# Chunked RWKV scan: which partition half each head's tiles live on, and how its stacked products are issued

## The chip, the cores and the metric

The kernel runs on one core of one Trainium2 chip. The metric is the device time of one execution in microseconds (us). A core has a tensor engine (PE, whose weight loads the profile lists apart as PEld), a vector engine (DVE), a scalar engine (ACT), a general engine (POOL), and SP, which issues transfers. Each engine works through its own queue in order and waits on semaphores.

## What is computed

The reference is a two-layer backbone over 512 tokens (256 of context, 256 latent). Each layer has a bidirectional RWKV-7 mixer, an attention, a Fourier mixer and a SwiGLU. The change touches the RWKV recurrence alone, which runs once in each direction for 8 heads of 64 features:

```python
def step(S, inp):
    r_t, w_t, k_t, v_t, kk_t, b_t = inp
    sa = -jnp.einsum("bhvk,bhk->bhv", S, kk_t)
    S = S * w_t[:, :, None, :] + sa[..., None] * b_t[:, :, None, :] + v_t[..., None] * k_t[:, :, None, :]
    return S, jnp.einsum("bhvk,bhk->bhv", S, r_t)
S, ys = lax.scan(step, state0, xs, reverse=reverse)
```

## The kernel before

All is float32. The kernel is a chain of stages, each a block with one program per engine. The stage `scan` (line 998) stands once in each layer. It does the recurrence in chunks of 64 tokens: 8 steps a layer, two directions `d` = 0 and 1 in each step, side by side. In the second layer the first 4 steps need no output `Y`.

Features are on partitions, two heads to a tile: head 2j on partitions 0 to 63 (`UP`), head 2j+1 on 64 to 127 (`DOWN`), so 4 pairs make 8 heads. PSUM is `BANK`; direction `d` owns four banks, 4d plus `B_L`, `B_LT`, `B_G`, `B_S`. One step does, in PE's order:

- **Gram products** (L1285 to L1291) of the scaled operands `BK` (keys) and `QR` (queries): `B_LT`, `B_L`, `B_G`, for d = 0 and then 1. ACT copies one of them to `LTS` (L1111) and the values to `VF` (L1114, each twice, 128x512). DVE masks them into the inverse's first level `T2` (L1198, L1200), and into `ARB` (L1204, one instruction a head half).
- **Transposes** of `BK` (L1296) and, behind ACT's copy `BK_TOK` (L1105), of `VF` (L1305).
- **Five levels** of the triangular inverse (L1298 to L1324): POOL masks `LM` (L1064), PE multiplies (`x1`), ACT copies `X1` (L1120), PE multiplies twice, DVE subtracts into `T2` (L1212, last level L1217). Between the levels DVE does `gram_out` (L1187) and `keep` (L1177), and the operands and exponents of the next step (L1168 to L1170, L1156, L1157); ACT the exponentials of the next step (L1088 to L1094) and copies of the values (L1129, L1134).
- **The end of the step**: `W` (L1333), the first part of `Y` (L1339), the solve (L1345), the rest of `Y` (L1351) and the new state product (L1360). ACT copies `W` (L1137) and `SA` (L1141, one instruction a head half); DVE adds `Y` (L1236) and updates the state: L1240 multiplies the product by the decay, L1243 adds `SD`, the decayed old state, which POOL made at the start of the step (L1056, L1057).

Three of these products contract over 128 partitions: tiles `QRG`, `STATE_V`, `SA_V`, `BK_TOK` hold, for each of 8 heads, the state, query or `SA` part on `UP` and the Gram, value or key part on `DOWN`. So 8 heads stand side by side in the free dimension (64 partitions x 512), and copies across halves are made one head half at a time. A product of 64 columns out goes to PSUM's upper or lower 64 partitions; L1333 and L1339 alternate between them, L1360 writes all heads to `UP`. A product with a contraction over 64 partitions (`each`, L1254) uses `UP` with `UP` and `DOWN` with `DOWN`, in turn. The profile shows two PE records for each float32 matmul.

Of the kernel before, what the change touches and what calls it, by code (L numbers as in the profile page):

```python
# [26 lines left out]
P = 128  # L27
# [8 lines left out]
HEADS = 8  # L36
# [143 lines left out]
def build_in(ctx, nc, ins, out):  # L180
# [30 lines left out]
    DEC = [sb(f"decay_{d}", [HD, HEADS]) for d in range(NDIR)]  # L211
    DEC_KEPT = [sb(f"decay_kept_{d}", [HD, HEADS]) for d in range(NDIR)]
# [694 lines left out]
    def scratch(*shape):  # L907
# [3 lines left out]
        for i, (mem, at, end) in enumerate(free):  # L911
            if at + n <= end:
# [9 lines left out]
    VF = [scratch(PAIRS, 2, HD) for _ in range(NDIR)]  # L922
    T2 = [scratch(2, PAIRS, HD) for _ in range(NDIR)]
    QRG = [scratch(HEADS, 2, HD) for _ in range(NDIR)]
    STATE_V = [scratch(HEADS, HD) for _ in range(NDIR)]
    SA_V = [scratch(HEADS, HD) for _ in range(NDIR)]
    BK_TOK = [scratch(HEADS, HD) for _ in range(NDIR)]
    ARB = [scratch(HEADS, HD) for _ in range(NDIR)]
    SD = [scratch(HEADS, HD) for _ in range(NDIR)]
# [30 lines left out]
    s_sa_v = [sig(f"values_doubled_{d}") for d in range(NDIR)]  # L960
# [3 lines left out]
    s_add = [sig(f"state_product_decayed_{d}") for d in range(NDIR)]  # L964
    s_ds = [sig(f"state_product_{d}") for d in range(NDIR)]
    s_y_out = [sig(f"y_added_{d}") for d in range(NDIR)]
    s_sd = [sig(f"state_decayed_{d}") for d in range(NDIR)]
# [6 lines left out]
    scan_signals = [s_expo, s_exp, s_init, *s_qr, *s_ops, *s_qr2, *s_gram, *s_lts, *s_gram_out, *s_bk_tok, *s_bk_turned, *s_v_turned, *s_add, *s_v, *s_v_tok, *s_sa_v, *s_lm, *s_x1, *s_x1_out,  # L974
                    *s_tx, *s_t, *s_w, *s_w_out, *s_sa, *s_sa_out, *s_y, *s_ds, *s_y_out, *s_sd, *s_st, *s_first, *s_arb]
# [22 lines left out]
    def scan(context_y):  # L998
# [30 lines left out]
        def of_head(h, half):  # L1029
# [4 lines left out]
        by_head = lambda tile, h: (tile.rearrange("p (j h) t -> p j h t", h=2)[:, :, h] if len(tile.shape) == 3 else  # L1034
                                   tile.rearrange("p (j h) q t -> p j h q t", h=2)[:, :, h])
        pairs = lambda bank, a: BANK[:, bank, a:a + HALF].rearrange("p (j t) -> p j t", j=PAIRS)
        with stage() as block:
            @block.gpsimd
            def _(pool):
# [9 lines left out]
                def step(i, need_y, more):  # L1049
                    t = [tokens(pool, d, i + 1) for d in range(NDIR)] if more else None  # L1050
                    for d in range(NDIR):

                        pool.wait_ge(*at_step(s_st[d], i))
                        pool.wait_ge(*at_step(s_exp, i, 2, d + 1))
                        hold(pool, "pool")
                        nc.gpsimd.tensor_copy(DEC_KEPT[d][:], DEC[d][:])  # L1056
                        s_sd[d].mark(nc.gpsimd.tensor_tensor(SD[d][UP], STATE_V[d][UP], DEC[d][:].unsqueeze(2).to_broadcast([HD, HEADS, HD]), ALU.mult))  # L1057
# [18 lines left out]
            def _(act):  # L1076
                def exps(i, t, d):
# [12 lines left out]
                    nc.scalar.activation(e[:, 2], incl, ACT.Exp, scale=KAPPA)  # L1090

                    act.wait_ge(*at_step(s_sd[d], i))
                    for h, rows in enumerate((UP, DOWN)):
                        last = nc.scalar.activation(DEC[d][:].rearrange("p (j h) -> p j h", h=2)[:, :, h:h + 1],  # L1094
                                                    INCL[d][rows, :, bass.ds(t + (CHUNK - 1), 1)], ACT.Exp, scale=-KAPPA)
                    s_exp.mark(last)

                def step(i, need_y, more):
                    here = [tokens(act, d, i) for d in range(NDIR)]
                    t = [tokens(act, d, i + 1) for d in range(NDIR)] if more else None  # L1100
                    def bk_token_major(d):

                        act.wait_ge(*at_step(s_bk_turned[d], i, 1, 1))
                        act.wait_ge(*at_step(s_ds[d], i))
                        s_bk_tok[d].mark(nc.scalar.activation(BK_TOK[d].rearrange("p g t -> p (g t)"), BANK[:, 4 * d + B_S], ACT.Copy))  # L1105

                    for d in range(NDIR):
                        act.wait_ge(*at_step(s_gram[d], i, 3, 1))
# [4 lines left out]
                        v_here = Z[:, Z_V:Z_V + PAIRS, bass.ds(here[d], CHUNK)]  # L1113
# [24 lines left out]
                    for d in range(NDIR):  # L1138
                        act.wait_ge(*at_step(s_sa[d], i, 1, 1))
                        for h, rows in enumerate((UP, DOWN)):  # L1140
                            last = nc.scalar.activation(by_head(SA_V[d][UP], h), pairs(4 * d + B_LT, 0)[rows], ACT.Copy, scale=-1.0)  # L1141
# [1157 lines left out]
```

## Time and profile before

| | us |
|---|---|
| median of 3 runs | 2362.63 |
| lowest, highest | 2360.34, 2364.29 |
| the profiled execution | 2364.6 |
| its span, first to last instruction | 2362.8 |

The page gives each engine's busy time and groups of instructions by line. The timeline gives instructions in order of time, where equal neighbours stand together as one row with their count, and in brackets the engine's idle time ahead of the row and what ended it. "Windows" give the busy time of each engine in a stretch, and the tensor clock granted in it (1.00 is the higher of its two levels, 2.4 GHz; 0.5 would be 1.2 GHz).

### The profile page before, as it was taken

To read this page: it belongs to the slowest core of one execution; us is meant where nothing else is said; L and a number is where in the kernel's file an instruction comes from. 1 tells how busy PE (TensorE), PEld (TensorE's weight loads), DVE (VectorE), ACT (ScalarE), POOL (GpSimd) and SP (SyncE) were. 2 spreads that over 40 slices of the span, in tenths; PEclk is the share of its full clock that TensorE was granted. 3 is DMA by queue.
4 is the path that set the end of the run, shared out by engine and by line. 5 is a ranking of instruction groups with operands and counts; after the bars stand their busy time and mean duration, and the time that the engine had idled before them with its cause. 6 is when DMAs were issued, how large, how long until landed. Compare 5 with 4: busy or idle time off the path is not lost. (4 is left out here: it accounts for less than half of the span.)

```text
span 2362.8 us, 46800 instructions
## 1 busy us (share of the span) xinstructions
PE 2087.1 (88%) x19559; PEld 1657.3 (70%) x19559; DVE 1169.0 (49%) x1849; ACT 832.9 (35%) x1515; POOL 340.5 (14%) x444
## 2 busy tenths in 40 slices
PE   4886888879989999889998998968888798988998
PEld 2653888843557887668886665748887456988988
DVE  1644778762562333253332216377877435545544
ACT  1343444423442222242221114354443244434432
POOL 1112333301100011010001001043332020010000
PEclk8997999989989999999999998979999899999999
DMA  7425000030111332223226743000001211553553
GB/s 263 152 85 200 1 0 2 1 127 13 36 51 49 92 106 89 72 71 107 90 89 238 282 154 125 27 2 0 1 1 44 96 36 56 170 179 125 185 172 126
DMA packets 144521, 219.40 MB, mean 93 GB/s; under 512 B 6846, under 2 KB 123800, under 8 KB 137216
## 3 DMA queue, kind: packets, MB, share of 16 engines
q1 hardware_dynamic: 142880, 215.74, 26.9%
q8 instruction: 101, 1.65, 0.3%
q0 software_dynamic: 1504, 1.71, 0.2%
q14 instruction: 36, 0.29, 0.0%
HBM read 208.00 MB, written 9.44 MB: 92 GB/s over the span
## 5 line engine op out<-in xcount | busy, mean ns | idle before, releaser
L367 PE MATMUL BANK<-H_high,W_high 128*128 128x512 f32 (+2 forms) x1472 | 524.2, 356 | 70.6 <-ACT H_high L630 32.3
L331 DVE TENSOR_TENSOR W_low<-RING,W_high 128x1024 fp32r<-128x1024 f32 x268 | 328.2, 1234 | 461.9 <-ACT W_high L328 461.9
L368 PE MATMUL BANK<-H_low,W_high 128*128 128x512 f32 (+2 forms) x1472 | 520.0, 353 | 0.0
L369 PE MATMUL BANK<-H_high,W_low 128*128 128x512 f32 (+2 forms) x1472 | 519.0, 353 | 0.0
L328 ACT ACTIVATE W_high<-RING 128x1024 fp32r<-128x1024 f32 x268 | 279.3, 1052 | 613.8 <-PE BANK L369 585.9
L367 PEld LDWEIGHTS BANK<-H_high,W_high 128*128 128x128 f32 (+1 forms) x1472 | 283.8, 193 | 117.0 <-issue 50.5
L368 PEld LDWEIGHTS BANK<-H_low,W_high 128*128 128x128 f32 (+1 forms) x1472 | 284.0, 193 | 38.0 <-issue 1.1
L369 PEld LDWEIGHTS BANK<-H_high,W_low 128*128 128x128 f32 (+1 forms) x1472 | 283.7, 193 | 38.0
L1259 PE MATMUL BANK<-RING,WORK 64*64 64x64 f32 x4096 | 166.4, 220 | 16.7 <-DVE RING L1212 8.8
L1259 PEld LDWEIGHTS BANK<-RING,WORK 64*64 64x64 f32 x4096 | 145.2, 134 | 29.2 <-issue 29.0
L1064 POOL TENSOR_TENSOR WORK<-WORK,masks 128x256 f32<-128x256 f32 x160 | 125.5, 796 | 116.5 <-PE BANK L1259 114.7
L367 PE MATMUL BANK<-hidden_high,W_high 128*128 128x512 f32 (+1 forms) x352 | 122.4, 348 | 12.0 <-PEq L2066 12.0
L368 PE MATMUL BANK<-hidden_low,W_high 128*128 128x512 f32 (+1 forms) x352 | 120.0, 341 | 0.0
L369 PE MATMUL BANK<-hidden_high,W_low 128*128 128x512 f32 (+1 forms) x352 | 120.0, 341 | 0.0
L1259 PE MATMUL BANK<-WORK,RING 64*64 64x64 f32 x2560 | 108.1, 225 | 3.1 <-issue 0.7
L2004 POOL TENSOR_TENSOR merge_tiles<-merge_tiles 128x512 f32<-128x512 f32 (+1 forms) x32 | 33.9, 1068 | 480.7 <-DVE merge_tiles L1986 480.7
L1120 ACT ACTIVATE WORK<-BANK 128x256 f32<-128x256 f32 (+1 forms) x160 | 56.5, 362 | 131.5 <-PE BANK L1259 123.5
L1259 PEld LDWEIGHTS BANK<-WORK,RING 64*64 64x64 f32 x2560 | 93.9, 139 | 8.3 <-issue 6.8
L1212 DVE TENSOR_TENSOR RING<-RING,BANK 128x512 f32<-128x512 f32 x128 | 83.7, 683 | 31.9 <-PE BANK L1259 29.1
L1259 PE MATMUL BANK<-RING 64*64 64x128 f32 (+1 forms) x1536 | 79.5, 263 | 21.1 <-DVE RING L1170 21.1
L367 PEld LDWEIGHTS BANK<-hidden_high,W_high 128*128 128x128 f32 x352 | 67.9, 193 | 34.9 <-issue 27.7
L1259 PEld LDWEIGHTS BANK<-RING 64*64 64x64 f32 x1536 | 75.6, 141 | 22.9 <-issue 21.9
(281 smaller groups left out, 3113.9 us busy)
## 6 DMA issues: line engine op xcount, KB each, us to landing
modulation_weights<-w_mod_dram SPq DMA_DIRECT2D x48, 1024.0 KB, 6.7
RING<-w_in_dram SPq DMA_DIRECT2D x46, 1024.0 KB, 5.9
RING<-w_ffn_in_dram SPq DMA_DIRECT2D x44, 1024.0 KB, 5.1
RING<-w_ffn_out_dram SPq DMA_DIRECT2D x20, 1024.0 KB, 5.1
RING<-w_out_dram SPq DMA_DIRECT2D x8, 1024.0 KB, 5.3
h_high<-H_high SPq DMA_DIRECT2D x2, 2048.0 KB, 7.5
h_low<-H_low SPq DMA_DIRECT2D x2, 2048.0 KB, 13.2
H_high<-h_high SPq DMA_DIRECT2D x2, 2048.0 KB, 11.8
```

The costliest lines, as they stand in the source:

```text
L328: high_ready.mark(nc.scalar.activation(self.part(0, c), self.raw(c), ACT.Copy))
L331: low_ready.mark(nc.vector.tensor_tensor(self.part(1, c), self.raw(c), self.part(0, c).bitcast(FP32), ALU.subtract))
L367: nc.tensor.matmul(out, w[0], x[0], start=start, stop=False)
L368: nc.tensor.matmul(out, w[0], x[1], start=False, stop=False)
L369: return nc.tensor.matmul(out, w[1], x[0], start=False, stop=stop)
L1064: s_lm[d].mark(nc.gpsimd.tensor_tensor(LM[d], LTS[d], lanes(level_mask(d, l)), ALU.mult))
L1120: s_x1_out[d].mark(nc.scalar.activation(X1[d][:, :, cols], pairs(4 * d + B_L, 0)[:, :, cols], ACT.Copy))
L1212: s_t[d].mark(nc.vector.tensor_tensor(T2[d].rearrange("p q j t -> p (q j t)"), T2[d].rearrange("p q j t -> p (q j t)"), BANK[:, 4 * d + B_ ...
L1259: last = nc.tensor.matmul(BANK[rows, bank, at + j * stride:at + j * stride + width], lhs(j)[rows], rhs(j)[rows], start=True, stop=True)
L2004: pool_sig.mark(nc.gpsimd.tensor_tensor(total(m), total(m), gate(u), ALU.add))
```

## The change

State, `SA`, `ARB` and the kept queries become tiles of 128 partitions x 4 pairs: each head's part stays on the half where its products arrive, so they are copied by one instruction of 128 partitions (`QR_KEPT`, `STATE`, `SA`, `ARB`). The Gram copy `GRAM_X` and the values `V_X` hold each head on the other half. Each product over 128 partitions becomes two over 64 that add up in PSUM: one from a head's own half (`OWN`), one from the other (`OTHER`). `side_by_side` issues an `OWN` and an `OTHER` product in turn, always into two banks, so that the four combinations of input half and output half follow each other. `B_LT` and `B_G` are issued so too. Where the two parts of one sum stand in one bank, the second waits for the first (`s_w_1`, `s_y_1`, `s_y_2`, `s_ds_1`, `s_turned_1`). The 128x128 transposes become products of 64x64 with a unit matrix. The state is first added to, then multiplied by the decay in place; `DEC_KEPT`, `SD` and POOL's two instructions go, and ACT makes the decay in levels 4 and 5 (`s_dec`).

```diff
-                        nc.gpsimd.tensor_copy(DEC_KEPT[d][:], DEC[d][:])
-                        s_sd[d].mark(nc.gpsimd.tensor_tensor(SD[d][UP], STATE_V[d][UP], DEC[d][:].unsqueeze(2).to_broadcast([HD, HEADS, HD]), ALU.mult))
...
-                        act.wait_ge(*at_step(s_gram[d], i, 3, 1))
+                        act.wait_ge(*at_step(s_gram[d], i, 3, 2))
...
-                            act.wait_ge(*at_step(s_v_tok[d], i, 1, 1))
-                            s_sa_v[d].mark(nc.scalar.activation(SA_V[d][DOWN].rearrange("p g t -> p (g t)"), BANK[DOWN, 4 * d + B_S], ACT.Copy))
+                            act.wait_ge(*at_step(s_st[d], i))
+                            s_dec[d].mark(nc.scalar.activation(DEC[d][:].unsqueeze(2), INCL[d][:, :, bass.ds(here[d] + (CHUNK - 1), 1)], ACT.Exp, scale=-KAPPA))
...
-                        for h, rows in enumerate((UP, DOWN)):
-                            last = nc.scalar.activation(by_head(SA_V[d][UP], h), pairs(4 * d + B_LT, 0)[rows], ACT.Copy, scale=-1.0)
-                        s_sa_out[d].mark(last)
+                        s_sa_out[d].mark(nc.scalar.activation(SA[d], pairs(4 * d + B_LT, 0), ACT.Copy, scale=-1.0))
...
-                        s_add[d].mark(nc.vector.tensor_tensor(STATE_V[d][UP], BANK[UP, 4 * d + B_S].rearrange("p (g t) -> p g t", g=HEADS),
-                                                              DEC_KEPT[d][:].unsqueeze(2).to_broadcast([HD, HEADS, HD]), ALU.mult))
+                        s_add[d].mark(nc.vector.tensor_tensor(STATE[d], STATE[d], pairs(4 * d + B_S, 0), ALU.add))
                         dve.wait_ge(*at_step(s_add[d], i, 1, 1))
-                        s_st[d].mark(nc.vector.tensor_tensor(STATE_V[d][UP], STATE_V[d][UP], SD[d][UP], ALU.add))
+                        dve.wait_ge(*at_step(s_dec[d], i, 1, 1))
+                        s_st[d].mark(nc.vector.tensor_tensor(STATE[d], STATE[d], DEC[d][:].unsqueeze(2).to_broadcast([P, PAIRS, HD]), ALU.mult))
...
+                OWN, OTHER = (UP, DOWN), (DOWN, UP)
+                def side_by_side(width, *products):
+
+                    last = [None] * len(products)
+                    for j in range(PAIRS):
+                        for x, (bank, at, rows, lhs, rhs, start, stop) in enumerate(products):
+                            for h in range(2):
+                                last[x] = nc.tensor.matmul(BANK[OWN[h], bank, at + j * width:at + (j + 1) * width], lhs(j)[rows[h]], rhs(j)[rows[h]],
+                                                           start=start and (j == 0 or stop), stop=stop and (j == PAIRS - 1 or start))
+                    return last
...
+                        for ins in side_by_side(2 * HD, (bank + B_LT, 0, OWN, lambda j: BK[d][:, j, 0], qr, True, True),
+                                                (bank + B_G, 0, OTHER, lambda j: BK[d][:, j, 1], qr, True, True)):
+                            s_gram[d].mark(ins)
...
+                    s_w_1.mark(side_by_side(HD, w_own(0, True), w_other(1, True))[1])
                     if need_y:
+                        s_y_1.mark(side_by_side(HD, y_own(0, True), y_other(1, True))[1])
+                    pe.wait_ge(*at_step(s_w_1, i, 1, 1))
+                    hold(pe)
+                    one, zero = side_by_side(HD, w_own(1, False), w_other(0, False))
+                    s_w[1].mark(one)
+                    s_w[0].mark(zero)
...
+                        solved, added = side_by_side(HD, (4 * d + B_LT, 0, OWN, lambda j: T2[d][:, 1, j], lambda j: WS[d][:, j], True, True),
+                                                     (4 * d + B_S, 0, OTHER, lambda j: BK_TOK[d][:, 1, j], lambda j: V_X[d][:, j], True, False))
```

The order on PE at the start of a step, before:

```order
L1259 MATMUL BANK<-RING 64x128 x8
L1259 MATMUL BANK<-RING 64x64 x8
L1259 MATMUL BANK<-RING 64x128 x16
L1259 MATMUL BANK<-RING 64x64 x8
L1259 MATMUL BANK<-RING 64x128 x8
L1296 MATMUL BANK<-ident,RING 128x128 x8
L1305 MATMUL BANK<-ident,RING 128x128 x4
```

and after (L1234 is `each`, L1247 `side_by_side`; the first rows are those of d = 0, up to the first transposes):

```order
L1234 MATMUL BANK<-RING 64x64 x8
L1247 MATMUL BANK<-RING 64x128 x16
L1247 MATMUL BANK<-eye_heads,RING 64x64 x16
L1234 MATMUL BANK<-RING 64x64 x8
L1247 MATMUL BANK<-RING 64x128 x16
L1247 MATMUL BANK<-eye_heads,RING 64x64 x24
```

The two wide Gram products of a direction now alternate in one run of 16, and half of the transposes stand between the directions. On DVE the state update stands last in the step, with `Y` ahead of it, before:

```order
L1236 ISA
L1236 TENSOR_TENSOR WORK<-WORK,BANK 128x4x64
L1240 TENSOR_TENSOR WORK<-BANK,decay_kept 64x512
L1243 TENSOR_TENSOR WORK<-WORK 64x512
L1240 TENSOR_TENSOR WORK<-BANK,decay_kept 64x512
L1243 TENSOR_TENSOR WORK<-WORK 64x512
```

and after:

```order
L1212 ISA
L1212 TENSOR_TENSOR WORK<-WORK,BANK 128x4x64
L1215 TENSOR_TENSOR RING<-RING,BANK 128x256
L1218 TENSOR_TENSOR RING<-RING,decay 128x256
L1215 TENSOR_TENSOR RING<-RING,BANK 128x256
L1218 TENSOR_TENSOR RING<-RING,decay 128x256
```

The places are the same; what moved is the layout: each instruction has all 128 partitions and half the elements in each.

## Rows read from the trace of the kernel before

**Rows 1.** Part 1 of the page: busy us, share of the span, instructions.

```profile
PE 2087.1 (88%) x19559; PEld 1657.3 (70%) x19559; DVE 1169.0 (49%) x1849; ACT 832.9 (35%) x1515; POOL 340.5 (14%) x444
```

**Rows 2.** Three steps by windows: length, busy us (instructions) of each engine, clock, DMA.

```profile
322.98:355.58 32.60, 29.22 (x722) 26.98 (x720) 24.49 (x42) 13.73 (x36) 11.71 (x16) 0.95 0.00 0
...
418.34:449.59 31.25, 27.73 (x722) 25.52 (x720) 24.50 (x43) 13.73 (x36) 11.71 (x16) 1.00 0.00 0
...
1633.66:1663.64 29.98, 26.89 (x658) 24.71 (x656) 23.67 (x41) 13.73 (x36) 11.71 (x16) 0.94 0.00 0
```

**Rows 3.** Line L1243 alone: ns least/median/most, first and last start.

```profile
L1243 DVE TENSOR_TENSOR WORK<-WORK x32: 682/684/1358, 258.4 to 1821.5; 64x512 f32<-64x512 f32 x32
```

**Rows 4.** Timeline, end of one step: start us, us, engine, line [idle before].

```profile
315.40 0.61 PE L1272 MATMUL BANK<-RING,WORK 32*32 32x32 f32 x32 [0.66 <-ACT WORK L1120]
...
315.94 1.15 PE L1333 MATMUL BANK<-WORK,RING 128*64 128x64 f32 x32
...
317.95 1.15 PE L1259 MATMUL BANK<-WORK,RING 64*64 64x64 f32 x32
318.68 1.56 ACT L1141 ACTIVATE WORK<-BANK 64x256 f32<-64x256 f32 x4 [1.16 <-PE BANK L1259]
...
321.00 2.08 PE L1360 MATMUL BANK<-WORK 128*64 128x64 f32 x32
321.42 0.42 DVE L1236 TENSOR_TENSOR WORK<-WORK,BANK 128x256 f32 x1 [0.47 <-PE BANK L1351]
...
323.01 3.19 PE L1259 MATMUL BANK<-RING 64*64 64x128 f32 x62
...
324.29 1.35 DVE L1243 TENSOR_TENSOR WORK<-WORK 64x512 f32<-64x512 f32 x1
```

**Rows 5.** Timeline, beginning of the same step.

```profile
291.75 4.64 PE L1259 MATMUL BANK<-RING 64*64 64x128 f32 x96
...
294.32 0.67 DVE L1198 TENSOR_TENSOR RING<-BANK,masks 128x512 f32<-128x512 f32 x1
...
295.03 2.03 DVE L1200 TENSOR_TENSOR RING<-RING,eye_heads 128x512 f32<-128x512 f32 x1
...
297.02 0.60 ACT L1105 ACTIVATE WORK<-BANK 128x512 f32<-128x512 f32 x1 [1.01 <-PE BANK L1296]
...
298.32 0.68 PE L1259 MATMUL BANK<-RING,WORK 64*64 64x64 f32 x16
...
299.42 0.68 PE L1259 MATMUL BANK<-RING,WORK 64*64 64x64 f32 x16 [0.42 <-DVE RING L1200]
```

**Rows 6.** Timeline, fourth and fifth level of that step.

```profile
312.54 0.41 DVE L1157 TENSOR_TENSOR WORK<-WORK 128x256 f32 x1
312.88 1.27 DVE L1212 TENSOR_TENSOR RING<-RING,BANK 128x512 f32<-128x512 f32 x2
...
314.36 0.59 ACT L1134 ACTIVATE WORK<-BANK 64x512 f32<-64x512 f32 x1
...
314.97 0.45 ACT L1120 ACTIVATE WORK<-BANK 128x128 f32<-128x128 f32 x2
```

**Rows 7.** Groups by line over the span: busy us, mean ns of one, idle before.

```profile
L1259 PE MATMUL BANK<-RING,WORK 64*64 64x64 f32 x4096 | 166.4, 220 | 16.7 <-DVE RING L1212 8.8 <-DVE RING L1200 4.6 <-issue 0.6
...
L1187 DVE TENSOR_TENSOR RING<-BANK,masks 64x512 f32<-64x512 f32 x64 | 44.1, 689 | 1.4
...
L1057 POOL TENSOR_TENSOR WORK<-WORK,decay 64x512 f32<-64x512 f32 x32 | 33.6, 1051 | 0.0
...
L1177 DVE COPY RING<-RING 64x512 f32<-64x512 f32 x64 | 31.8, 497 | 1.4
...
L1204 DVE TENSOR_TENSOR WORK<-BANK,masks 64x256 f32<-64x256 f32 x64 | 26.6, 416 | 0.4
...
L1272 PE MATMUL BANK<-RING,WORK 32*32 32x32 f32 x1024 | 24.7, 194 | 19.8 <-ACT WORK L1120 9.6 <-DVE RING L1212 9.3
```

**Rows 8.** Groups by line, stage before the scan, 200.0 to 200.5 us.

```profile
L449 PE MATMUL BANK<-modulation_weights,condition_padded 128*32 128x512 f32 x8 | 1.1, 604 | 1.8 <-DMA modulation_weights<-w_mod_dram 1.8
```

More of the change, by code:

```diff
@@ L921, in build_in @@
     BK = [scratch(PAIRS, 2, HD) for _ in range(NDIR)]
-    VF = [scratch(PAIRS, 2, HD) for _ in range(NDIR)]
+    VF = [scratch(PAIRS, HD) for _ in range(NDIR)]
     T2 = [scratch(2, PAIRS, HD) for _ in range(NDIR)]
[L924 to L929, printed above, removed]
+    QR_KEPT = [scratch(PAIRS, 2, HD) for _ in range(NDIR)]
+    GRAM_X = [scratch(PAIRS, 2, HD) for _ in range(NDIR)]
+    STATE = [scratch(PAIRS, HD) for _ in range(NDIR)]
+    V_X = [scratch(PAIRS, HD) for _ in range(NDIR)]
+    SA = [scratch(PAIRS, HD) for _ in range(NDIR)]
+    BK_TOK = [scratch(2, PAIRS, HD) for _ in range(NDIR)]
+    ARB = [scratch(PAIRS, HD) for _ in range(NDIR)]
     EXPO = scratch(2, PAIRS, HD)
@@ L1284, in step @@
                         hold(pe)
-                        s_gram[d].mark(each(bank + B_LT, 0, 2 * HD, lambda j: BK[d][:, j, 0], qr))
                         s_gram[d].mark(each(bank + B_L, 0, HD, q, lambda j: BK[d][:, j, 0], 2 * HD))
@@ L1290, in step @@
                         hold(pe)
-                        s_gram[d].mark(each(bank + B_G, 0, 2 * HD, lambda j: BK[d][:, j, 1], qr))
-                    for d in range(NDIR):
-                        pe.wait_ge(*at_step(s_add[d], i))
-                        hold(pe)
-                        for j in range(PAIRS):
-                            last = nc.tensor.transpose(BANK[:, 4 * d + B_S, j * P:(j + 1) * P], BK[d][:, j].rearrange("p q t -> p (q t)"), ident[:])
-                        s_bk_turned[d].mark(last)
+                        for ins in side_by_side(2 * HD, (bank + B_LT, 0, OWN, lambda j: BK[d][:, j, 0], qr, True, True),
+                                                (bank + B_G, 0, OTHER, lambda j: BK[d][:, j, 1], qr, True, True)):
+                            s_gram[d].mark(ins)
+                        if d == 0:
+                            pe.wait_ge(*at_step(s_add[0], i))
+                            pe.wait_ge(*at_step(s_add[1], i))
+                            pe.wait_ge(*at_step(s_ops[1], i, 1, 1))
+                            pe.wait_ge(*at_step(s_qr[1], i, 1, 1))
+                            hold(pe)
+                        turned = side_by_side(HD, (B_S + 4 * d, 0, OWN, lambda j: BK[d][:, j, 0], eye, True, True),
+                                              (B_S + 4 * (1 - d), HALF, OTHER, lambda j: BK[1 - d][:, j, 1], eye, True, True))
+                        if d == 0:
+                            s_turned_1.mark(turned[1])
+                            pe.wait_ge(*at_step(s_turned_1, i, 1, 1))
+                            hold(pe)
+                        else:
+                            s_bk_turned[1].mark(turned[0])
+                            s_bk_turned[0].mark(turned[1])
                     for l in range(1, LEVELS):
@@ L1303, in step @@
                             hold(pe)
-                            for j in range(PAIRS):
-                                last = nc.tensor.transpose(BANK[:, 4 * d + B_S, j * P:(j + 1) * P], VF[d][:, j].rearrange("p q t -> p (q t)"), ident[:])
-                            s_v_turned[d].mark(last)
+                            turned = side_by_side(HD, (4 * d + B_S, 0, OTHER, lambda j: VF[d][:, j], eye, True, True))
+                            s_v_turned[d].mark(turned[0])
                         for d in range(NDIR):
```

97 lines of the change are left out of this document (36 added, 61 removed).

## Prediction

> **What bounds the kernel now.** I read part 1 of the page first: PE is busy for 88% of the span [rows 1]. That share is a mean over stages, and the change touches the scan alone, so the next view is the timeline of one step of the scan, taken from one start of the Gram products to the next. L1243, twice in each step, is found 32 times, so there are 16 steps, the first ending near 258 and the last near 1821 us, with the rest of layer one between them [rows 3]. Three steps read as windows say what one costs: 31.25 us with `Y` (12 of the 16), 29.98 without (4), and 32.60 where the granted clock was 0.95 instead of 1.00 [rows 2]. So the scan is about 12 x 31.3 + 4 x 30.0 = 495 us of the 2363, and no DMA bounds it.
>
> I cut the step at three points: Gram products start at 291.75, the first level product at 298.32 [rows 5], `W` at 315.94 and the next Gram products at 323.01 [rows 4] (the step that ends there is the one that began at 291.75): **head** 6.57, **levels** 17.62, **end** 7.07 us, 31.26 in all. In the head PE finishes its Gram products after 4.64 us, but the first level starts 1.9 us later. What is late there is DVE: it runs L1198, then 2.03 us of L1200, and direction 1's first level product starts only 1.10 us after direction 0's [rows 5]; DVE is late because the state update before it ran to 325.64 (324.29 + 1.35), 2.6 us into the next step [rows 4]. In the levels PE, ACT and DVE take turns, and in several of them DVE is late: at 312.88 it starts L1212 as soon as L1157 is off it, with no idle time in front [rows 6]. In the end PE and ACT alternate, and PE is nearly always at work [rows 4].
>
> **What PE pays for a tile.** Each float32 matmul is two records. 16 matmuls that alternate between the two output halves take 1.15 us up to the end of the last, whose latency is 0.22 [rows 4, 7]: 0.93, or 0.47 for 8. L1360, with as many matmuls and elements but one output half only, takes 2.08 [rows 4]. So two tiles run at once where the output halves differ. Four at once are seen too: L449 puts four tiles of 32 output columns beside each other, and its 8 records, 0.60 us each in the mean, are over in 1.1 us, 4.8 us of work in 1.1 [rows 8]. And L1272's last run passes 32 records in 0.61 us, of which 0.19 is the latency of the last [rows 4, 7]: 13 ns a record. What no row shows is two tiles with different input halves and the **same** output half. I take it that they run together, as L449's do: a set of 16 matmuls of `side_by_side` then costs what 8 cost now, 0.47 (4 records in 58 ns, 15 ns each, above the 13 seen). The other end is 0.94, two at a time.
>
> The Trainium skill bears against this: its page TensorEngine Tiling (Array Packing), section Performance Considerations, gives each matmul an overhead of about 60 cycles, which is an estimated 25 ns at 2.4 GHz. By that a set (32 records) would take 0.80 and not 0.47, and the gain would be about 1.7 us a step, 27 in all, a harder case of rival 2. The 13 ns a record of L1272 speak against it here.
>
> The same page, section Restrictions and Gotchas, says that row tiles may not be in the same PSUM bank at one time. The sets always use two banks; no run here shows what else would happen.
>
> **The end, 7.07 now.** `W` and the first `Y` are four sets, in the order W, Y, W, Y: both W's are there after 3 x 0.47 + 0.20 latency = 1.61 (now direction 0's is there after 0.68: a loss of 0.9, which today the `Y` run in front of the solve hides, since PE reaches L1259 only at 317.95, 2.01 after the start). ACT's copy of 0.4 gives 2.05, and the fourth set lies under it. The solve of direction 0 with the first part of the state product is 0.47, and its result is there at 2.77. The copy of `SA` is one instruction instead of two for each direction: 0.38, 0.38 against the 1.56 for four [rows 4]; they end at 3.2 and 3.65. The rest of `Y` is 0.94, from 3.3 to 4.25. The state product is two runs of 8 over both output halves, 0.94 in place of L1360's 1.98, to 5.2. With 0.2 for the first records after each wait: **5.4, a gain of 1.7**.
>
> **The head, 6.57 now.** PE: 0.47 (`B_L`) + 0.87 (`B_LT` and `B_G` as one set of 128 columns; one such product alone takes the same now: 4.64 us are 2 x (0.87 + 0.47 + 0.87) and latency) + 0.47 (transposes) + 0.2 (wait for `s_turned_1`) + 0.47 + 0.87 + 0.2 = 3.55 until ACT may copy direction 1's. Then ACT's `LTS` 0.38 and `VF` about 0.4, `BK_TOK` 0.60 [rows 5], PE's transpose of the values 0.47, and handing over between them: 5.6. DVE must keep up: its state update is 4 x 0.42, as L1236 of the same shape [rows 4], with no POOL instruction beside it. It now takes 0.68, 0.68, 0.68 and 1.35, and ends 1.5 after the Gram products start instead of 2.6. Then L1198 0.67 and L1200, which takes 2.03 beside POOL's L1057 (1.05 each) [rows 5, 7] and should take 0.69. `ARB` is one instruction of 0.42 for two. Direction 1's level product then starts 0.5 after direction 0's and no longer 1.10. **5.6, a gain of 0.97.** What is late next is ACT's chain of three copies behind the second Gram set.
>
> **The levels, 17.62 now.** `gram_out` goes from 2 x 0.689 to one of 0.69, `keep` from 2 x 0.497 to one of about 0.45 [rows 7]: 1.2 us less of DVE in each of levels 1 and 2. I walked the levels with the products at 0.47 for 8, ACT's copy 0.38, DVE's 0.69 and POOL untouched: 3.4, 3.7, 3.4, 4.3 and 1.7 us, which is 0.35, 0.2 and 0.45 less than now in the first three, 0.35 more in the fourth and 0.45 less in the last. The fourth loses, since the gain before it brings its `L1212` forward and direction 1's does not come forward as far, and since the next step's operands and exponents (up to L1157 at 312.54 [rows 6]) still stand ahead of L1212 there. The last gains since ACT's L1134 (0.59) no longer stands ahead of L1120, which waited until 314.97 [rows 6]; the decay there is 0.2. Sum 16.5, **a gain of 1.1**.
>
> Together 1.7 + 0.97 + 1.1 = 3.8 us a step. Without `Y` the end is 5.8 now and 4.3 then (the wait for `s_w_1`, 0.2, is open there), so 3.6. 12 x 3.76 + 4 x 3.6 = 59.5 us. The profiled execution took 2364.6, 2.0 above the median of the three runs; 2364.6 - 59.5 = 2305, and against the median 2303. I say **2304**.
>
> Two edits cost nothing: the decay on ACT replaces L1094, at a time when ACT waits for PE, and PE's 80 matmuls more a step lie in sets that are costed. If their cover goes, the first costs 0.2 a step.
>
> **Rival 1, slower.** Two tiles that share an output half do not run together; the place is every set of `side_by_side`, and the price 0.47 more for each set of 64 columns and 0.87 for each of 128. The end becomes 7.8 (three sets to both W's, 2.8 + 0.2, and the solves 0.94 each, against a state product that is 0.94 shorter), the head 7.9 (two wide sets at 1.75, transposes at 0.94), the levels stay at 16.5: +0.9 a step, +15 us, **2377**. It decides against the change as soon as a set of 16 takes more than about 0.84 us. For it: no row shows the pair. Against it: L449 and L1272, with four tiles.
>
> **Rival 2, half the gain.** The records of a set come slower than 15 ns, say midway to today's 29: 21 ns, 0.68 a set. Four sets of the end and two of the head lie on the path: +1.3 a step, so a gain of 2.5, 40 us, **2323**. For it: L1272's run is only 32 records long.
>
> **Rival 3, the clock.** PE was granted less than full clock in one short stretch in some steps, and such a step is 1.35 us longer [rows 2]. If the new step has such a stretch every time, 16 x 1.35 = 21 us are given back: **2325**. For it: PE works less in each step and waits for ACT's chain in the head. Against: the steps as a whole shorten by as much as the work does.
>
> **The numbers.** Forecast as stated, give or take 15 us (each of the three gains wrong by a quarter): 0.62. Rival 2 or 3, or both in part, 2318 to 2345: 0.23. Rival 1: 0.11. A gain well over 75 us: 0.04. The range, 2286 to 2345, holds the first two. A measurement of this kernel can tell 0.2% (4.7 us) from no change. Faster 0.86, same 0.03, slower 0.11.
>
> **What would show it.** Right: steps of 27.5 us; a set of 16 matmuls of 64 columns at a spacing of about 0.47 us; the Gram products of a step begun 5.4 after `W`; L1179, the new L1200, near 0.69 and not 2.03; POOL without a state instruction. Wrong: sets at 0.9 us (rival 1), 0.7 (rival 2), windows of a step with a clock below 1.00 in nearly all of them (rival 3), or DVE without idle time ahead of L1177 in the head, which would mean that the state update still sets the head.

## The result: slower by 1.8%, and the profile after

The changed kernel took 2404.68 us (median of 4 runs, 2402.31 to 2409.67), the kernel before beside it 2361.78 (4 runs, 2360.34 to 2364.29): a ratio of 1.0183, interval 1.0165 to 1.0202. The forecast was 2304, the range ended at 2345, and even the slower rival stood at 2377. The spans of the two profiled executions are 2407.5 and 2362.8 us, so 44.7 us have to be found.

Part 1 of the page of after, against [rows 1], and from part 3 of both pages the queue that carries instructions (packets, MB, share of the DMA engines), first after, then before:

```profile
PE 2071.7 (86%) x22247; PEld 1642.9 (68%) x22247; DVE 1075.5 (45%) x1753; ACT 774.1 (32%) x1419; POOL 298.1 (12%) x380
...
q8 instruction: 172, 2.82, 0.5%
```

```profile
q8 instruction: 101, 1.65, 0.3%
```

Every engine has less work than in [rows 1]: PE 15 us less, DVE 93, ACT 59, POOL 42. None of them became the bound by being busy for longer. What grew is the code that was brought in while the kernel ran: 71 packets more, of 16 KB each.

Next, windows of after (columns as in [rows 2]): a step with `Y` in the middle of the first scan's first loop, the first trip of its second loop, the scan's last step, a step without and one with `Y` of the second scan, the whole first and second scan from first to last state update, and all that comes behind.

```profile
296.19:334.11 37.92, 27.38 (x896) 25.22 (x896) 18.42 (x37) 10.09 (x30) 8.97 (x12) 0.91 0.02 4
371.36:404.82 33.46, 25.39 (x893) 23.31 (x892) 18.12 (x37) 10.20 (x30) 8.79 (x12) 1.00 0.01 4
483.22:515.37 32.15, 26.10 (x895) 24.10 (x891) 14.40 (x29) 8.22 (x24) 7.22 (x10) 0.95 0.02 4
1665.53:1692.58 27.05, 23.20 (x807) 21.48 (x805) 17.74 (x34) 10.09 (x30) 9.10 (x12) 0.99 0.00 0
1751.71:1788.28 36.57, 27.57 (x896) 24.88 (x896) 18.41 (x36) 10.09 (x30) 8.97 (x12) 0.95 0.02 4
259.57:515.37 255.80, 191.49 (x6272) 177.02 (x6272) 124.99 (x245) 68.84 (x204) 61.40 (x82) 0.91 0.02 4
1637.25:1858.40 221.15, 181.90 (x5992) 168.00 (x5988) 122.73 (x238) 68.77 (x204) 61.34 (x82) 0.94 0.01 2
1858.40:2407.50 549.10, 488.49 (x3400) 430.23 (x3400) 266.75 (x409) 215.42 (x338) 32.82 (x46) 0.95 0.39 128
```

The same three long stretches of the kernel before:

```profile
258.44:479.74 221.30, 198.25 (x5049) 182.75 (x5047) 165.99 (x287) 93.67 (x242) 80.01 (x110) 0.98 0.00 1
1603.63:1820.15 216.52, 193.51 (x4850) 178.33 (x4848) 165.18 (x280) 93.66 (x242) 80.22 (x110) 0.97 0.00 1
1820.15:2362.80 542.65, 483.12 (x3402) 424.96 (x3400) 268.00 (x409) 215.58 (x338) 32.90 (x46) 0.95 0.40 129
```

The first scan is 34.5 us longer, the second 4.6, the stages behind it 6.5; what lies ahead of the first scan and between the two is 0.9 shorter together. That makes the 44.7. And the scans differ in kind. A step with `Y` takes 36.6 to 40.0 us in the middle of a loop, with PE busy for only 27.4 of 37.9: it idles for 10.5 us, where it idled for 3.5 in [rows 2]. A step without `Y`, in the same kernel and with the same layout, takes 27.05, for a forecast of 26.4. The last columns tell them apart: 4 GB/s of DMA against 0. The traffic in the slow step, in the step without `Y` and its neighbours (1637.25 to 1720.19 us, where a queue other than q8 carried the one packet), and in two steps of the kernel before:

```profile
q8 instruction: 9, 0.15, 1.6%
```

```profile
DMA packets 1, 0.01 MB, mean 0 GB/s; under 512 B 0, under 2 KB 0, under 8 KB 0
```

```profile
DMA packets 0, 0.00 MB, mean 0 GB/s; under 512 B 0, under 2 KB 0, under 8 KB 0
```

So in after the steps with `Y` bring in packets of instructions, 9 in this one and 7 to 10 in the others, and a step of before brings in none (once 1) except where the loop over steps changes its body, where 5 or 6 come in. Where the step loses its time, by the timeline of PE in after (start us, us, engine, line, what, [idle before, what ended it]) and by its waits over that step (us in total, times, longest):

```profile
299.46 0.62 PE L1234 MATMUL BANK<-RING 64*64 64x64 f32 x14 [3.60 <-issue]
...
302.67 1.22 PE L1247 MATMUL BANK<-RING 64*64 64x128 f32 x17 [2.08 <-issue]
```

```profile
PE BANK L1234 <- issue: 3.9, 2, 3.6
PE BANK L1247 <- issue: 3.6, 3, 2.1
```

The Gram products start 3.60 us late, and the second set, in the middle of a run of matmuls that wait for no engine, stops for another 2.08. "issue" means that PE waited for nothing that the profile shows. In all these are 7.5 us of the step; DVE, ACT and POOL wait for PE meanwhile.

### The profile page after: what moved, and what is told of

It reads as the page before. It is cut to its first block and busy times, and to the rows that moved or that the text cites. A ratio compares the mean times of both kernels' runs of the same rounds, so it can differ in the third digit from the quotient of the medians.

```text
span 2407.5 us, 51837 instructions
## 1 busy us (share of the span) xinstructions
PE 2071.7 (86%) x22247; PEld 1642.9 (68%) x22247; DVE 1075.5 (45%) x1753; ACT 774.1 (32%) x1419; POOL 298.1 (12%) x380
## 3 DMA queue, kind: packets, MB, share of 16 engines
q1 hardware_dynamic: 142880, 215.74, 26.4%
## 5 line engine op out<-in xcount | busy, mean ns | idle before, releaser
L367 PEld LDWEIGHTS BANK<-H_low,W_high 128*128 128x128 f32 (+1 forms) x1472 | 284.2, 193 | 37.9 <-issue 1.1
L1234 PE MATMUL BANK<-RING,WORK 64*64 64x64 f32 x4096 | 170.4, 220 | 12.1 <-issue 4.1
L1234 PEld LDWEIGHTS BANK<-RING,WORK 64*64 64x64 f32 x4096 | 146.8, 135 | 21.8 <-issue 21.2
L1247 PE MATMUL BANK<-RING 64*64 64x128 f32 (+1 forms) x1920 | 89.1, 291 | 10.7 <-issue 8.6
L1234 PE MATMUL BANK<-WORK,RING 64*64 64x64 f32 x2048 | 86.9, 220 | 2.8 <-issue 0.8
L1247 PEld LDWEIGHTS BANK<-RING 64*64 64x64 f32 x1920 | 74.8, 164 | 14.9 <-issue 14.8
L1234 PE MATMUL BANK<-RING 64*64 64x64 f32 x512 | 28.7, 263 | 58.0 <-issue 31.1
```

What stands on the lines that cost most here:

```text
L367: nc.tensor.matmul(out, w[0], x[1], start=False, stop=False)
L1234: last = nc.tensor.matmul(BANK[rows, bank, at + j * stride:at + j * stride + width], lhs(j)[rows], rhs(j)[rows], start=True, stop=True)
L1247: last[x] = nc.tensor.matmul(BANK[OWN[h], bank, at + j * width:at + (j + 1) * width], lhs(j)[rows[h]], rhs(j)[rows[h]], start=start and (j ...
```

## The experiments

**Theory.** PE's loop body for a step with `Y` grew from 368 to 448 matmuls, transposes counted in. At 448 it is no longer kept from one trip of the loop to the next, so PE fetches it again in every trip and stands still meanwhile; the new layout itself is as fast as forecast. **Rivals.** The layout causes the stalls in another way (banks, tiles side by side, the order of the waits); or the gain was never there.

These counts are those of the code. The expectations below give each of them seven lower (361, 441 and so on): 361 is half of the 722 PE records of [rows 2], but each of before's 16 transposes has one record and not two, while after does that work with matmuls of two. The loop body of before is 1440 records of PE and PEld together, that of after 1792 with `Y` and 1600 without.

### 1. The changed kernel with a loop over three levels

PE's part of levels 1 to 3 becomes a loop of three trips. The work is the same, but the body holds 352 matmuls with `Y` and 304 without. Direction 1's values are transposed behind level 3 instead of ahead of it, and the wait for `ARB` stands in every level.

```diff
-                    for l in range(1, LEVELS):
-                        if l in (1, 3):
...
+                    turn_values(0)
+                    trips = Signal.trips
+                    Signal.trips = 3 * trips
+                    with pe.Fori(1, 4) as l:
+                        level(l, False)
+                    Signal.trips = trips
+                    turn_values(1)
+                    level(4, False)
+                    level(5, True)
```

> The changed kernel, with PE's first three levels of the inverse written as one loop of three trips (the values of direction 1 are turned after it): the same matmuls are executed in nearly the same order, but a step's body on PE shrinks from 441 matmuls to 345 (345 is below the 361 of the kernel before). Theory 1 (PE's loop body with Y, 441 matmuls, is too long to be kept, so its code is fetched again in every step and PE stands still for it): instruction packets of 16 KB vanish inside the loops, steps with Y take 27 to 28.5 us and not 37, the total is 2300 to 2325 us. Theory 2 (the new order of the W and Y sets and their waits cost the time in steps with Y): no difference, 2400 to 2410 us. Theory 3 (lower clock takes the time): steps stay over 33 us, as the clock follows from the same work.

Measured: 2338.42 us (4 runs, 2335.04 to 2342.64) against 2364.96 of before, ratio 0.9889 (0.9873 to 0.9906). That is slower than the 2300 to 2325 expected of this run, though the step came out as expected. The change turns from 1.8% slower to 1.1% faster by how PE's code is written. Windows: a step with `Y` and one without, the first step of the loop's second body in each scan, both scans, and the stages behind:

```profile
287.59:315.61 28.02, 24.89 (x905) 23.39 (x903) 18.53 (x37) 10.21 (x30) 9.13 (x12) 1.00 0.00 0
1611.23:1638.84 27.61, 23.25 (x800) 21.43 (x801) 18.18 (x34) 10.21 (x30) 9.13 (x12) 1.00 0.00 0
344.66:374.74 30.08, 24.74 (x878) 22.90 (x874) 18.53 (x37) 10.21 (x30) 8.86 (x12) 1.00 0.01 3
1667.54:1699.95 32.41, 26.53 (x907) 24.81 (x904) 18.68 (x36) 10.21 (x30) 9.09 (x12) 0.97 0.01 3
259.47:461.76 202.29, 177.54 (x6265) 166.32 (x6261) 125.84 (x244) 69.44 (x204) 61.22 (x82) 0.98 0.00 1
1583.06:1784.59 201.53, 172.72 (x5991) 160.91 (x5988) 124.95 (x239) 69.44 (x204) 61.94 (x82) 0.98 0.00 1
1784.59:2332.90 548.31, 488.88 (x3400) 429.88 (x3400) 266.93 (x409) 215.69 (x338) 32.88 (x46) 0.96 0.39 128
```

The step is 28.0 us, where after had 37.9, and its clock is 1.00 instead of 0.91. Of the 11 steps with `Y` in the two scans 8 have 1.00, one 0.97 and two 0.94; in after they have 0.83 to 1.00. So most of after's lower clock came with PE standing still.

### 2. The same loop in the kernel before

The same edit on the old kernel (272 matmuls with `Y`, instead of 368).

```diff
+                    with pe.Fori(1, 4) as l:
+                        level(l, False)
...
+                    turn_values(1)
+                    level(4, False)
```

> The kernel before, with the same loop of three trips on PE: body 265 matmuls instead of 361, nothing else changed. Theory 1: the body of before is kept already, so nothing is gained; the loop's branches may cost up to 0.3 us a step, total 2362 to 2368 us. If the loop alone were a gain whatever the body's length (another reason than code length), this kernel would be faster than before by as much as the other one against the changed kernel.

Measured: 2364.47 us, ratio 0.9997 (0.9987 to 1.0007). The step is as long as the 31.25 of [rows 2]:

```profile
291.74:323.03 31.29, 27.67 (x722) 25.51 (x720) 24.54 (x42) 13.71 (x36) 11.66 (x16) 1.00 0.00 0
```

So the loop has no worth and no cost of its own, within 0.13%, where the code is small enough anyway, and the gain of experiment 1 does not come from it.

### 3 and 4. The kernel before with 80 more matmuls, written out and in a loop

Direction 0's first product of level 1 (8 matmuls) is repeated ten times more. It writes what is there already, so nothing else changes. Once the 80 matmuls are written out, which gives the old kernel the 448 of after (1760 records for 1792):

```diff
+                                if l == 1 and d == 0:
+                                    for _ in range(10):
+                                        x1()
```

> The kernel before, with the first level product of direction 0 repeated ten times more (80 matmuls, 2.3 us of PE work a step), written out: the body with Y is as long as that of the changed kernel (441 matmuls), the one without Y is 409. The result is not altered. Theory 1: steps with Y pay some 4 to 8 us beyond the padding's own 2.3 us and show 8 or 9 instruction packets each; steps without Y (409) pay 2.3 only if 409 is still kept. Theory 2 or 3: every step pays 2.3 us and no more, about 2400 us in all.

and once they stand in a loop of ten trips (376 matmuls in the code, 448 run):

```diff
+                                if l == 1 and d == 0:
+                                    with pe.Fori(0, 10):
+                                        x1()
```

> The same 80 matmuls a step as in the padded kernel, executed by a loop of ten trips over 8: the work is the same, the body is only 369 and 337 matmuls long. Theory 1: no instruction packets inside the loops, every step costs about 2.3 to 3 us more than before, about 2400 to 2410 us, and the difference to the written-out one is the price of fetching: 12 steps less two last ones, x 5 us, some 50 us. Theory 2 or 3: the same time as the written-out one within 5 us.

Measured: 2485.91 us and 2445.75 us (one run each). The second was expected at 2400 to 2410: the expectation priced the 80 matmuls at 2.3 us a step, and their 160 records of 29 ns are 4.6. Windows of the first: a step with `Y`, one without (416 matmuls) that fetched its code, and one without that brought in a single packet, with the traffic of the first two:

```profile
307.24:351.19 43.95, 34.28 (x876) 31.90 (x875) 23.26 (x42) 13.72 (x36) 11.29 (x16) 0.95 0.02 4
1710.98:1751.85 40.87, 33.22 (x818) 31.00 (x816) 22.42 (x40) 13.72 (x36) 11.28 (x16) 0.92 0.01 3
1751.85:1786.49 34.64, 31.59 (x818) 29.49 (x816) 23.67 (x41) 13.73 (x36) 11.64 (x16) 0.95 0.00 0
```

```profile
q8 instruction: 10, 0.16, 1.7%
```

```profile
q8 instruction: 7, 0.11, 1.1%
```

Windows of the second, a step with `Y` and one without, and the traffic of the step with `Y`:

```profile
303.23:340.33 37.10, 33.88 (x882) 31.66 (x880) 24.49 (x43) 13.73 (x36) 11.64 (x16) 0.95 0.00 0
1682.38:1717.05 34.67, 31.55 (x818) 29.45 (x816) 23.68 (x40) 13.73 (x36) 11.64 (x16) 0.95 0.00 0
```

```profile
DMA packets 0, 0.00 MB, mean 0 GB/s; under 512 B 0, under 2 KB 0, under 8 KB 0
```

The same 448 matmuls run in both, with the old layout and without any step in which four tiles work. Written out they cost 6.9 us more in the step with `Y` (43.95 against 37.10); over the kernel it is 40 us, for some 50 expected. In the step without `Y` it is 6.2 where 7 packets came in and nothing where one did. The waits of PE in the slow step are of the kind seen in after:

```profile
PE BANK L1259 <- issue: 4.7, 2, 3.0
PE BANK L1343 <- issue: 1.9, 1, 1.9
```

That is 6.6 of the 6.9 us. The rival that the layout makes the stalls falls with this pair: the old layout has them as well, as soon as the code has that length.

What costs time here is not that code is brought in, but when. The next rows are two neighbouring steps with `Y` of the written-out kernel, the first trip of the second loop and the trip behind it:

```profile
393.62:429.51 35.89, 32.61 (x882) 30.27 (x880) 23.81 (x43) 13.73 (x36) 11.65 (x16) 1.00 0.01 3
429.51:471.53 42.02, 35.31 (x882) 32.89 (x880) 23.24 (x43) 13.73 (x36) 11.30 (x16) 0.92 0.01 4
```

The first trip, which PE reaches without jumping back, brings in 7 packets of q8 and has no wait on "issue" at all. The second brings in 9 and has 3.5 us of it. So here the standstill comes with the jump back to the start of a body that is no longer there.

### 5. Sixteen matmuls fewer: where the edge is

The same with eight repeats instead of ten: 432 matmuls with `Y` (1696 records), and 400 without (1568).

```diff
-                                    for _ in range(10):
+                                    for _ in range(8):
```

> The kernel before, with the first level product of direction 0 repeated 8 times more, written out (64 matmuls, 1.9 us of work a step): the bodies are 425 matmuls with Y, 393 without. The changed kernel showed no packets in its loop with 393 and 9 a step with 441; the padded one with 409 in the second layer had 8 in one of three steps. If the code length decides: the steps without Y have no packets and take about 33 us; those with Y have 8 or 9 packets and over 39 us if 425 is too long, or 34 to 35 us if it is still kept. The result is not altered.

Measured: 2469.04 us (one run). A step with `Y` and one without, and the traffic of the first and of the stretch 1674 to 1773 us, which holds only steps without `Y`:

```profile
308.36:350.83 42.47, 35.17 (x850) 32.46 (x848) 22.38 (x43) 13.84 (x36) 11.27 (x16) 0.92 0.02 3
1707.64:1740.97 33.33, 30.61 (x786) 28.48 (x784) 23.67 (x40) 13.73 (x36) 11.66 (x16) 0.95 0.00 0
```

```profile
q8 instruction: 9, 0.15, 1.7%
```

```profile
DMA packets 0, 0.00 MB, mean 0 GB/s; under 512 B 0, under 2 KB 0, under 8 KB 0
```

Over all kernels, by records of PE and PEld: bodies of up to 1600 (after without `Y`) were kept in every trip, the one of 1632 brought in 7 packets in one step of three and 2 and 1 in the others, and those of 1696, 1760 and 1792 were lost in every trip.

### 6. One loop instead of two

All engines run the 8 steps as loops of 4 and 3 trips and a last step written out by itself. Here PE alone runs one loop of 8 trips in layer one and two of 4 in layer two, so fewer bodies are fetched for the first time.

```diff
-                run(pe, step)
+                for first, end, need_y in (((0, STEPS, True),) if context_y else ((0, N, False), (N, STEPS, True))):
+                    Signal.trips = end - first
+                    with pe.Fori(first, end) as i:
+                        step(i, need_y, True)
+                    Signal.trips = 1
```

Once on experiment 1's kernel:

> The kernel with the level loop, and in addition PE runs its 8 steps of a scan in one loop (first layer) or two of four trips (second layer) instead of two loops and a last step written out: 3 bodies of PE code in the program for 6, the same matmuls. In the kernel with the level loop 5 instruction packets come in at each change from one body to the next, and the step in which that happens takes 30.1 and 32.4 us against 28.1. If PE's code fetching costs there too: 2 to 4 us less for each of the changes that go, total 2326 to 2336 us against 2338. If those steps are long for another reason (clock, the first Y): no difference.

Measured: 2335.05 us (4 runs, 2321.16 to 2336.86), ratio 0.986 (0.9824 to 0.9895), too wide to tell it from experiment 1. Together with the same edit on the kernel before (with experiment 2's loop) it was run once more:

> The changed kernel with both loops on PE, measured again in more rounds, since one of its four runs was 2321 us and the others 2334 to 2337. Expected 2333 to 2337 us, 0.986 to 0.988 of before, and no instruction packet of PE inside the loops.

> The kernel before with both loops on PE, the level loop and one or two loops for the steps of a scan: the control for the fastest version. If the loops alone were worth something, it would be faster than before by more than 0.1%. Theory 1 expects little: before's code is kept inside its loops, and its steps at a change of body took 31.5 and 32.9 us against 31.3, so 2358 to 2365 us, and the gain of the fastest version comes from the change itself.

Measured: 2331.18 us (4 runs, 2329.12 to 2332.65), ratio 0.9866 (0.985 to 0.9883), for 2333 to 2337 expected, and 2362.49, ratio 0.9994 (0.9984 to 1.0004). Windows of the first: a step with `Y`, one without, the first step of the second body in layer two, and both scans:

```profile
316.92:344.93 28.01, 24.88 (x904) 23.38 (x902) 18.54 (x37) 10.21 (x30) 9.13 (x12) 1.00 0.00 0
1608.63:1635.81 27.18, 23.32 (x800) 21.58 (x801) 17.77 (x35) 10.21 (x30) 9.14 (x12) 1.00 0.00 1
1664.77:1694.64 29.87, 25.67 (x922) 24.02 (x922) 18.54 (x36) 10.21 (x30) 9.14 (x12) 1.00 0.01 3
260.71:457.18 196.47, 175.02 (x6270) 164.51 (x6265) 125.90 (x245) 69.49 (x204) 62.22 (x82) 0.99 0.00 0
1581.46:1777.76 196.30, 171.58 (x5984) 160.24 (x5984) 123.65 (x239) 69.51 (x204) 62.22 (x82) 0.98 0.00 1
```

Fewer bodies take 5.8 and 5.2 us off the two scans of experiment 1's kernel, and the span is 5.9 shorter (2327.0 for 2332.9). The worth of this edit is not shown firmly: the times of the second set do not overlap experiment 1's (up to 2332.65, from 2335.04), those of the first set do (up to 2336.86), and the intervals of the ratios overlap as well. In the kernel before it gives nothing measurable. By its median this is the fastest version: 33 us under the kernel before it was run with.

### 7. Are four tiles at once real?

Experiment 1's kernel with `side_by_side` issuing one product behind the other, instead of both in turn. All instructions are the same; two tiles are at work at a time.

```diff
-                    for j in range(PAIRS):
-                        for x, (bank, at, rows, lhs, rhs, start, stop) in enumerate(products):
+                    for x, (bank, at, rows, lhs, rhs, start, stop) in enumerate(products):
+                        for j in range(PAIRS):
```

> The kernel with the level loop, but side_by_side issues all matmuls of its first product and then all of the second, so that two tiles run at a time and not four; the same matmuls, the same code length. If four tiles really run at once in the sets (0.47 us for 16): the narrow sets take 0.94 and the wide ones 1.75, steps with Y 31.5 to 33 us and not 28.1, total 2385 to 2410 us. If the gain of the sets came only from the layout of the copies: no difference, 2338.

Measured: 2366.8 us (one run), 28 more than experiment 1. A step with `Y`, by its window:

```profile
291.67:322.32 30.65, 27.89 (x904) 26.54 (x901) 18.53 (x37) 10.31 (x30) 9.12 (x12) 0.94 0.00 0
```

The step is 2.6 us longer, less than the 3.4 to 4.9 expected (the total was expected at 2385 to 2410), and a part of it is the clock, 0.94 against 1.00. But the set itself shows the effect: the 32 records of the first transposes start 27 ns apart here (323.49 to 324.33 us), and 15 ns apart in experiment 1 (288.51 to 288.98). And with the products no longer in turn the whole gain of the layout over the kernel before is gone (2366.8 against 2364.7): four tiles at once are real, and the gain rests on them.

### 8. Was it POOL that made DVE late?

Experiment 1's kernel with a POOL instruction of the removed one's size put back behind the state update, in a tile that nobody reads, and DVE's wait for it before the next state update.

```diff
+                    for d in range(NDIR):
+                        pool.wait_ge(*at_step(s_st[d], i))
+                        hold(pool, "pool")
+                        s_sd[d].mark(nc.gpsimd.tensor_tensor(SD[d][UP].rearrange("p (j h) t -> p j h t", h=2), STATE[d][UP].unsqueeze(2).to_broadcast([HD, PAIRS, 2, HD]),
...
+                        dve.wait_ge(*at_step(s_sd[d], i, 1, 1))
```

> The kernel with the level loop, with an instruction of 64x512 on POOL for each direction behind the state update, as the kernel before had one (here it multiplies the state by itself into a tile that nobody reads), and the wait of the next state update for it. The theory of the head says that DVE's state and first-level instructions get slower beside it (0.42 to about 0.8, 0.69 to 1.3 or 2.0) but that the chain over ACT's three copies has up to about 1 us to spare over DVE: steps 0 to 1 us longer, total 2338 to 2356 us. If DVE alone set the head before, the step loses about 1.5 to 2 us, 2362 to 2370 us.

Measured: 2339.24 us (2 runs), ratio 0.9893 (0.9873 to 0.9912), the same as experiment 1. DVE's groups over the first scan (busy us, mean ns of one) in experiment 1's kernel, the copy of the Gram products (there L1179, which was L1200 in [rows 5]) and the state's multiply, and then the same two with the POOL instruction back:

```profile
L1179 DVE TENSOR_TENSOR RING<-RING,eye_heads 128x512 f32<-128x512 f32 x14 | 9.7, 692 | 0.5
...
L1218 DVE TENSOR_TENSOR RING<-RING,decay 128x256 f32<-128x256 f32 x16 | 6.8, 425 | 0.5
```

```profile
L1186 DVE TENSOR_TENSOR RING<-RING,eye_heads 128x512 f32<-128x512 f32 x14 | 13.4, 960 | 0.5
L1226 DVE TENSOR_TENSOR RING<-RING,decay 128x256 f32<-128x256 f32 x16 | 11.7, 733 | 0.5
```

```profile
319.70:347.71 28.01, 24.87 (x906) 23.39 (x904) 19.65 (x36) 10.20 (x30) 11.57 (x14) 1.00 0.00 0
```

POOL does slow DVE, by 268 and 308 ns an instruction, and the step is 28.01 all the same: in the new layout DVE has that much to spare. Taking POOL's instruction out was worth nothing that can be measured here (0.8 us between the medians).

## Why the prediction was wrong

**The step that failed** is this one: "Two edits cost nothing: [...] PE's 80 matmuls more a step lie in sets that are costed." Their time on PE was costed; their code was not. The step's body on PE went from 368 to 448 matmuls, and PE did not keep it: 7 to 10 packets of 16 KB come in during each step with `Y`, and in the step shown PE stands still for 7.5 us. None of the three rivals held this either. The slower rival put the loss in tiles that would not run together, and the one on the clock saw the lower clock as a thing by itself.

How much it cost: 2404.68 against 2338.42 of experiment 1, **66 us** for the same work (the kernel before beside them differs by 3). By steps it is 37.9 against 28.0. Of these 9.9, 7.5 are PE's waits on "issue"; the rest, I take it, is the clock (0.91 against 1.00), which I have not measured apart. The old layout paid 6.9 for nearly the same length of code (experiments 3 and 4). That after paid more may be because its sets get through a packet of code in half the time (15 ns a record for 29), so that less of the fetching lies beside work. In line with that, the first trip of the second loop (371.36 to 404.82 us in after), which the padded kernel passes without a standstill, has 5.1 us of "issue" in after; no run tests it apart.

A look at the kernel before would have hinted at it. The views of its trace give 0 packets in a step inside a loop and 5 or 6 in the first step of a body, so that its 1440 records come in as 6 packets, or 96 KB. The Trainium skill has a size to hold 80 more against: its page Advanced Engine Details and Errata, section ISA Cache, gives TensorE 128 KB, in lines of 16 KB with 256 instructions. The packets here have that size and the trace agrees so far: after's 1792 records and the 56 waits, counts, branches and register instructions that its trace has for PE in that step are 1848 instructions, an estimated 7.2 lines of that page or 116 KB. That would still fit in the 128 KB, and it was not kept: the edge to go by is the measured one, between 1600 records and 1696. The page is not refuted by this, since a trip brings in up to 10 packets, more than its 128 KB hold; why it brings in more than the body has is open.

**The terms of the sum**, by the timeline of PE in experiment 1's kernel, cut at the same places as in [rows 4, 5]: Gram products, the transposes of the first set, first level product, and the next Gram products:

```profile
287.17 0.62 PE L1234 MATMUL BANK<-RING 64*64 64x64 f32 x14
...
288.51 0.69 PE L1247 MATMUL BANK<-eye_heads,RING 64*64 64x64 f32 x32
...
293.04 1.15 PE L1234 MATMUL BANK<-RING,WORK 64*64 64x64 f32 x32
```

```profile
315.19 0.62 PE L1234 MATMUL BANK<-RING 64*64 64x64 f32 x14
```

`W` starts at 309.62 in the same timeline.

- **A set of 16 matmuls, 0.47 us**: right. The transposes are 32 records in 0.69, of which 0.22 is the latency of the last. The 25 ns that the prediction estimated from the Trainium skill (TensorEngine Tiling (Array Packing), section Performance Considerations) was rightly set aside as the spacing of such records: 15 ns were measured.
- **Head 5.6**: 5.87. One reason given for it made no difference, though: DVE's L1179 does fall to 0.69, but experiment 8 puts it back to 0.96 in the mean (at most 1.13) at no cost. ACT's chain of three copies is what is late, as was said; whether it would have hidden the 2.03 of [rows 5] too no run shows.
- **Levels 16.5**: 16.6. **End 5.4**: 5.6, and without `Y` 4.7 for 4.3.
- **Step 27.5**: 28.0 with `Y`, against the 31.25 of [rows 2]; 27.2 to 27.6 without, for 26.4.
- **59.5 us in all**: this does not hold even without the fetching. Experiment 1's 2338.42 would have been inside the range, but its gain is 26.5 us. The two scans' windows (14 of the 16 steps) are shorter by 19.0 and 15.0 us in experiment 1's kernel and 24.8 and 20.2 in experiment 6's, where the forecast's share of them is 52.1. Of the 7 us missing in the latter, steps of 28.0 for 27.5 and 27.2 for 26.4 account for all (7.9); in the former 11 us more are missing, of which the steps in which a new body is fetched (30.1 and 32.4 instead of 28) are 6.5, and three steps at a clock of 0.92 to 0.94 (29.05 and 29.46 with `Y`, 28.70 without) 3.6. The two steps ahead of the windows were forecast to gain 7.4 together and gave 1.5 in experiment 1's kernel, with what else lies in those stretches, and in experiment 6's those stretches are 2.7 longer.
- **What lies behind the scans** was taken as untouched, and is 4.5 to 6.6 us longer than before's 542.65 in every kernel with the new layout (547.1 to 549.3); with the old one it is 541.7 to 545.3, the last of these with the 80 matmuls in a loop. It is the same with the code written out and in a loop, so the length of the body does not explain it. Two stretches hold most of it, and the last of them (2310.0 to 2362.8 us in before, 2352.1 to 2407.5 in after) shows of what kind it is: 407 matmuls in both, PE busy for 46.17 and 48.78 us, the clock 0.99 in both. So the matmuls themselves come more slowly, and PE does not wait longer. Why is **open**: no run tests it. The tiles of the scan became smaller, and no run shows whether that moved what these stages read.

**Clock.** Rival 3 was about a stretch below full clock in each step. In experiment 1's kernel the clock is 1.00 in 8 of 11 steps with `Y`, and the two at 0.94 are 1.0 and 1.4 us longer than the 28.02 of the step shown. Such steps occur as they do in before, but not every time, so the rival did not come about.

## What to carry to other kernels

Count an engine's instructions between two ends of a loop before adding any, as one counts bytes in a buffer: on PE each float32 matmul is four records here, and a body of 1600 was the longest that stayed. Look in the trace of the kernel as it is for instruction packets in a step in the middle of a loop (none means that the body is kept, and the packets of a body's first trip tell its size), and for idle time that "issue" ends inside a run of matmuls. Where the body is near the edge, a loop over equal inner parts cost nothing measurable (experiment 2), and it decided here between 1.8% slower and 1.1% faster; where the body fits anyway, it gives nothing.

## What the runs showed of the chip that I had not expected

- The loss sets in within 6% of length: bodies of 1568 and 1600 records fetched next to nothing in the trips behind their first, and one of 1696 fetched 8 or 9 packets in each, up to 144 KB, which is more than the body itself.
- Bringing in code is not by itself what costs: the padded old kernel took in 7 packets without a standstill in the first trip of a body and stood still for 3.5 us in the next trip, behind the jump back. In after the first trip cost time too, but less (33.46 us against 36.6 to 40.0).
- A body just at the edge (1632 records) is lost in some trips and nearly kept in others: 40.87 us with 7 packets and 34.64 with one, in successive steps of one loop.
- A loop of ten trips over eight matmuls cost PE nothing to be seen: the step of experiment 4 is 37.10 us with the clock at 0.95, where before's is 32.60 at 0.95 [rows 2], and the 80 matmuls are 160 records of 29 ns, or 4.6.
- The clock is lower where PE stands still to fetch: after's steps with `Y` in the middle of a loop have 0.83 to 0.95, those of the same work in a shorter body 0.94 to 1.00.
